# Attention inside a two-layer trunk: score matmuls in pairs of unlike row halves, values as the stationary operand, the softmax division ahead of the transposes

## The reference

```python
s_loc = jnp.einsum('bqgrd,bkgd->bgrqk', qb, kb).astype(jnp.float32) * scale
...
s_ctx = jnp.einsum('bqgrd,bkgd->bgrqk', qc, ck).astype(jnp.float32) * scale
p = jax.nn.softmax(jnp.concatenate([s_loc, s_ctx, sink_b], axis=-1), axis=-1)
o = (jnp.einsum('bgrqk,bkgd->bqgrd', p[..., :span].astype(v.dtype), vb)
     + jnp.einsum('bgrqk,bkgd->bqgrd', p[..., span:span + P].astype(cv.dtype), cv))
```

## Time and profile before

| | us |
|---|---|
| median of 3 runs | 1668.3 (1663.09 to 1668.85) |
| the profiled execution's own time | 1660.22 |
| its span | 1658.4 |
| mean granted PE clock | 0.91 of full speed |
| PE busy | 1321.3 (80% of the span) |
| DVE busy | 520.7 (31%) |
| ACT busy | 390.9 (24%) |
| POOL busy | 277.5 (17%) |

### The profile page before, as it was taken

One profiled execution on the slowest core, in us unless ns is written; L12 is line 12 of the kernel. 1 busy time (PEld: TensorE's weight loads), 2 busy tenths in 40 slices (PEclk: granted clock), 3 DMA queues, 4 the chain that ended last, 5 costly groups with the idle time before them and its releaser, 6 DMA issues.

```text
span 1658.4 us, 16936 instructions
## 1 busy us (share of the span) xinstructions
PE 1321.3 (80%) x6726; PEld 778.6 (47%) x6726; DVE 520.7 (31%) x1042; ACT 390.9 (24%) x753; POOL 277.5 (17%) x279
## 2 busy tenths in 40 slices
PE   3899989967996788989881799898699677787770
PEld 1455565545344344655440466565555444444430
DVE  3327542254123332121003285434622510000005
ACT  4311133211213122221123311332013311111113
POOL 4210010002000133232222026000000022222222
PEclk9899997988997699999995899899799679999995
DMA  9748110053555399999986021002000459999974
GB/s 347 254 158 285 53 54 26 26 191 130 190 175 209 125 415 419 395 415 381 394 365 228 0 76 55 0 26 83 32 0 39 177 204 417 400 412 407 406 297 195
DMA packets 71697, 350.90 MB, mean 212 GB/s; under 512 B 12925, under 2 KB 21755, under 8 KB 36680
## 3 DMA queue, kind: packets, MB, share of 16 engines
q1 hardware_dynamic: 56188, 316.78, 49.0%
q0 software_dynamic: 12704, 22.03, 3.7%
q10 hardware_dynamic: 2732, 11.08, 1.7%
HBM read 334.36 MB, written 31.20 MB: 220 GB/s over the span
## 4 chain that ended last, share of the span: by engine, by line
PE 57%; DMA 22%; DVE 11%; ACT 6%; issue 3%; SPq 0%; ACTq 0%; POOL 0%; POOLq 0%; DVEq 0%
DMA ring<-in_exp_up 17%; PE ps L1294 10%; PE ps L1241 9%; PE ps L1081 5%; PE ps L987 4%; PE ps L1309 3%; PE ps L1038 3%; PE ps L848 2%; PE ps L1008 2%; PE ps L1143 2%; DMA ring<-in_ada_w 2%; PE ps L1190 2%; PE ps L901 1%; PE ps L1221 1%; PE ps L1088 1%
## 5 line engine op out<-in xcount | busy, mean ns | idle before, releaser
L1294 PE MATMUL ps<-ring,work 128*64 128x256 f32 x2176 | 256.6, 389 | 47.6 <-DMA ring<-in_exp_up 44.5
L1294 PEld LDWEIGHTS ps<-ring,work 128*64 128x64 f32 x2176 | 173.2, 140 | 154.5 <-issue 95.3
L1309 PE MATMUL ps<-ring,work 128*64 128x512 f32 x544 | 133.5, 612 | 26.1 <-DVE work L2153 21.5
L1241 PE MATMUL ps<-ring,yT 128*128 128x512 f32 x320 | 145.2, 603 | 0.8 <-issue 0.8
L2151 DVE TENSOR_TENSOR work<-work,ps 64x256 f32<-64x256 f32 x56 | 23.8, 424 | 345.8 <-ACT work L1665 345.8
L780 POOL DMA_INDIRECT y_scratch<-work,tabs x56 | 57.7, 1030 | 337.1 <-ACT work L1672 337.1
L1911 DVE SCALAR_TENSOR_TENSOR work<-work,prmT 128x655 f32<-128x655 f32 x120 | 97.7, 891 | 0.0
L1241 PEld LDWEIGHTS ps<-ring,yT 128*128 128x128 f32 x320 | 59.5, 193 | 75.1 <-issue 75.0
L775 POOL DMA_INDIRECT work<-h_scratch,tabs x60 | 61.8, 1029 | 194.8 <-issue 157.2
L1081 PE MATMUL ps<-hT,ring 128*128 128x512 f32 x192 | 91.7, 622 | 0.3
L987 PE MATMUL ps<-hT,ring 128*128 128x512 f32 x128 | 68.0, 613 | 3.4 <-POOL hT L741 1.9
(11 more groups left out here) (375 smaller groups left out, 1886.3 us busy)
## 6 DMA issues: line engine op xcount, KB each, us to landing
ring<-in_exp_gate SPq DMA_DIRECT2D x68, 1024.0 KB, 8.1
ring<-in_exp_up SPq DMA_DIRECT2D x68, 1024.0 KB, 12.5
ring<-in_exp_down SPq DMA_DIRECT2D x68, 1024.0 KB, 11.8
ring<-in_ada_w SPq DMA_DIRECT2D x48, 1024.0 KB, 4.8
ring<-in_w_in SPq DMA_DIRECT2D x16, 1024.0 KB, 6.9
work<-y_scratch SPq DMA_DIRECT2D x10, 1024.0 KB, 6.8
ring<-in_w_out SPq DMA_DIRECT2D x8, 1024.0 KB, 6.3
k_scratch<-yT ACTq DMA_DIRECT2D x4, 1280.0 KB, 8.0
```

Of the source, the lines that this page charges most:

```text
L1241: last = mm(ps[:, (4, 6, 7, 0)[n % 4], :], yT[:, k, t * P:(t + 1) * P], wo[k // 2][:, k % 2, h * HALF:(h + 1) * HALF], start=(k == 0), sto ...
L1294: last = mm(ps[BR * q:BR * q + BR, 1, 0:FE], xe[:, s, kb, BR * h:BR * h + BR], w[:, q, k, :], start=(k == 0), stop=(k == KC - 1))
L1309: last = mm(ps[BR * h:BR * h + BR, 3, :], he[:, s, k, :], wd[:, k, HALF * h:HALF * h + HALF], start=(k == 0), stop=(k == 1))
```

## The change

- **Scores.** `score(i, h)` becomes `scores(i, m)`, which does the two heads m and m + 2 together: the matmul against the cached keys on rows 0 to 63, the same on rows 64 to 127, then the two against the rotated keys, again one on each half. Two of these pairs are placed behind the transposes of heads 2 and 3.
- **Values.** The values are stationary (128x64) and the transposed probabilities of two heads are streamed (256 columns). The matmul for key/value head 0 writes partitions 0 to 63 of bank 6, that for head 1 partitions 64 to 127; they alternate. The result is already transposed, so the two transposes of `otok`, `otok` itself and the semaphore `at_ot` are gone, and ACT copies `yT` from bank 6 after `at_pv`. PE waits for `yd_ok` ahead of the values, no longer ahead of head 1.
- **Division.** `divide(i)` on DVE now scales `prob` in place, per head, in two groups of two heads, before the transposes; these wait for `at_o` (20 per layer) in place of `at_exp`. It stands between `maximum(i)` and `outer_taps(i)`.
- **Output weights.** The heads now lie in another order in `yT`, so the last quarter of `w_out` is loaded in two DMAs of 64 partitions with its rows in that order, and `w_count` counts the extra one.

```diff
@@ out_unit (SP)
+                if j == 3:
+                    w = io["w_out"][l][3 * CH:4 * CH, :].rearrange("(g r d) n -> g d r n", g=2, r=2)
+                    for g in range(2):
+                        sp.dma_start(wbuf(OUT_U + j, 2, D)[g * HD:(g + 1) * HD], w[g]).then_inc(w_full[j % 4], 16)
+                    return
@@ PE
-                def score(i, h):
+                def scores(i, m):
                     if i > 0:
-                        pe.wait_ge(at_exp, nth(l, at_exp, 4 * (i - 1) + h + 1))
-                    p0, m = HD * (h // 2), h % 2
+                        pe.wait_ge(at_exp, nth(l, at_exp, 4 * (i - 1) + m + 3))
+                    lo, hi = max(i - 1, 0), min(i + 2, 4)
+                    for g in range(2):
+                        p0 = HD * g
+                        if i < 4:
+                            mm(ps[:, 2 * g + m, 0:P], qraw[p0:p0 + HD, m, i * P:(i + 1) * P], ckT[p0:p0 + HD, :],
+                               start=True, stop=True)
+                        else:
+                            mm(ps[:, 2 * g + m, 0:P], qraw[p0:p0 + HD, m, LS:T], kraw[p0:p0 + HD, LS:T],
+                               start=True, stop=True).then_inc(at_s, 1)
                     if i < 4:
-                        lo, hi = max(i - 1, 0), min(i + 2, 4)
-                        mm(ps[:, h, 0:P], qraw[p0:p0 + HD, m, i * P:(i + 1) * P], ckT[p0:p0 + HD, :], start=True, stop=True)
-                        last = mm(ps[:, h, P:P + (hi - lo) * P], qrope[p0:p0 + HD, m, i * P:(i + 1) * P],
-                                  krope[p0:p0 + HD, lo * P:hi * P], start=True, stop=True)
...
+                        for g in range(2):
+                            p0 = HD * g
+                            mm(ps[:, 2 * g + m, P:P + (hi - lo) * P], qrope[p0:p0 + HD, m, i * P:(i + 1) * P],
+                               krope[p0:p0 + HD, lo * P:hi * P], start=True, stop=True).then_inc(at_s, 1)
...
                     for h in range(4):
-                        pe.wait_ge(at_exp, nth(l, at_exp, 4 * i + h + 1))
-                        if h == 1 and i > 0:
-                            pe.wait_ge(yd_ok, nth(l, yd_ok, i))
+                        pe.wait_ge(at_o, nth(l, at_o, 4 * i + h + 1))
                         if h >= 2:
                             pe.wait_ge(at_te, nth(l, at_te, 4 * i + h - 1))
                         for t in range(nk):
                             last = tr(ps[:, 4 + h % 2, t * P:(t + 1) * P], prob[:, h, t * P:(t + 1) * P], ident)
                         last.then_inc(at_t, 1)
-                        if i + 1 < NT:
-                            score(i + 1, h)
+                        if i + 1 < NT and h >= 2:
+                            scores(i + 1, h - 2)
                     hyena_tile(i + 1, 0, 4)
-                    for h in range(4):
-                        kv = h // 2
-                        pe.wait_ge(at_te, nth(l, at_te, 4 * i + h + 1))
-                        for t in range(nk):
+                    pe.wait_ge(at_te, nth(l, at_te, 4 * i + 4))
+                    if i > 0:
+                        pe.wait_ge(yd_ok, nth(l, yd_ok, i))
+                    for t in range(nk):
+                        for kv in range(2):
...
-                            last = mm(ps[:, 6, h * HD:(h + 1) * HD], probT[:, h, t * P:(t + 1) * P], v,
+                            last = mm(ps[kv * HD:(kv + 1) * HD, 6, 0:2 * P], v, probT[:, 2 * kv:2 * kv + 2, t * P:(t + 1) * P],
                                       start=(t == 0), stop=(t == nk - 1))
                     last.then_inc(at_pv, 1)
                     hyena_tile(i + 1, 4, KC)
-                    pe.wait_ge(at_o, nth(l, at_o, i + 1))
-                    for q in range(2):
-                        last = tr(ps[:, 5, q * P:(q + 1) * P], otok[:, q * P:(q + 1) * P], ident)
-                    last.then_inc(at_ot, 1)
@@ ACT
-                    act.wait_ge(at_ot, nth(l, at_ot, i + 1))
-                    A(yT[:, 6:8, i * P:(i + 1) * P], ps[:, 5, 0:2 * P].rearrange("p (q t) -> p q t", q=2), ACT.Copy) \
+                    act.wait_ge(at_pv, nth(l, at_pv, i + 1))
+                    A(yT[:, 6:8, i * P:(i + 1) * P], ps[:, 6, 0:2 * P].rearrange("p (q t) -> p q t", q=2), ACT.Copy) \
@@ DVE, divide(i)
-                    dve.wait_ge(at_exp, nth(l, at_exp, 4 * i + 4))
-                    step(V.tensor_tensor(ast[:, i % 2, 6, :], ast[:, i % 2, 3, :], ast[:, i % 2, 4, :], ALU.add))
-                    step(V.reciprocal(ast[:, i % 2, 7, :], ast[:, i % 2, 6, :]))
-                    dve.wait_ge(at_pv, nth(l, at_pv, i + 1))
-                    V.tensor_tensor(otok.rearrange("p (h c) -> p h c", h=4), ps[:, 6, 0:256].rearrange("p (h c) -> p h c", h=4),
-                                    bc(ast[:, i % 2, 7, :], HD), ALU.mult).then_inc(at_o, 1)
+                    nk = (3, 4, 4, 3, 1)[i]
+                    for a in (0, 2):
+                        dve.wait_ge(at_exp, nth(l, at_exp, 4 * i + a + 2))
+                        step(V.tensor_tensor(ast[:, i % 2, 6, a:a + 2], ast[:, i % 2, 3, a:a + 2], ast[:, i % 2, 4, a:a + 2],
+                                             ALU.add))
+                        step(V.reciprocal(ast[:, i % 2, 7, a:a + 2], ast[:, i % 2, 6, a:a + 2]))
+                        for h in (a, a + 1):
+                            V.tensor_scalar(prob[:, h, 0:nk * P], prob[:, h, 0:nk * P], ast[:, i % 2, 7, h:h + 1], None,
+                                            ALU.mult).then_inc(at_o, 1)
@@ DVE, the loop
                 outer_taps(0)
+                divide(0)
                 for i in range(NT):
                     if i + 1 < NT:
                         maximum(i + 1)
-                    divide(i)
+                        divide(i + 1)
                     outer_taps(i + 1)
```

More of the change, by code:

```diff
@@ L193, in trunk @@
         probT = at(work, 3584, 4, 512)
-        otok = at(work, 5632, 256)
         u = ([yT[:, 2 + c, :] for c in range(2)] + [at(ring[:, 5, :], i * T, T) for i in range(3)]
@@ L357, in trunk @@
         at_o = sem("at_o")
-        at_ot = sem("at_ot")
         yd_ok = sem("yd_ok")
@@ L459, in trunk @@
             (at_mm, 5), (at_ev, 8), (at_rot, 3), (at_rope, 3), (kv_out, 32), (at_s, 20), (at_max, 5), (at_exp, 20),
-            (at_t, 20), (at_te, 20), (at_pv, 5), (at_o, 5), (at_ot, 5), (yd_ok, 5),
+            (at_t, 20), (at_te, 20), (at_pv, 5), (at_o, 20), (yd_ok, 5),
             (hy_lay, 3), (hy_phase, 2), (hy_sine, 2), (hy_f, 10), (hy_raw, 10), (hy_abs, 10), (hy_eo, 10), (hy_norm, 2),
@@ L483, in w_count @@
         def w_count(l, j):
-            return 16 * (2 + 3 * l + j // 4)
+            return 16 * (2 + 3 * l + j // 4) + 16 * ((j % 4 == 3) * l + (j == OUT_U + 3))
         apos = [(4, 5, 0, 1, 2, 3)[p] if p < 6 else 4 if 24 <= p < 32 else 4 + p % 2 for p in range(24 * DEPTH)]
@@ L1098, in _ @@
                 pe.wait_ge(hy_uc, nth(l, hy_uc, 1))
-                def score(i, h):
+                def scores(i, m):
                     if i > 0:
-                        pe.wait_ge(at_exp, nth(l, at_exp, 4 * (i - 1) + h + 1))
-                    p0, m = HD * (h // 2), h % 2
-                    if i < 4:
-                        lo, hi = max(i - 1, 0), min(i + 2, 4)
-                        mm(ps[:, h, 0:P], qraw[p0:p0 + HD, m, i * P:(i + 1) * P], ckT[p0:p0 + HD, :], start=True, stop=True)
-                        last = mm(ps[:, h, P:P + (hi - lo) * P], qrope[p0:p0 + HD, m, i * P:(i + 1) * P],
-                                  krope[p0:p0 + HD, lo * P:hi * P], start=True, stop=True)
-                    else:
-                        last = mm(ps[:, h, 0:P], qraw[p0:p0 + HD, m, LS:T], kraw[p0:p0 + HD, LS:T], start=True, stop=True)
-                    last.then_inc(at_s, 1)
-                for h in range(4):
-                    score(0, h)
+                        pe.wait_ge(at_exp, nth(l, at_exp, 4 * (i - 1) + m + 3))
[8 more added lines that the diff above has]
+                               start=True, stop=True).then_inc(at_s, 1)
+                    if i < 4:
+                        for g in range(2):
+                            p0 = HD * g
+                            mm(ps[:, 2 * g + m, P:P + (hi - lo) * P], qrope[p0:p0 + HD, m, i * P:(i + 1) * P],
+                               krope[p0:p0 + HD, lo * P:hi * P], start=True, stop=True).then_inc(at_s, 1)
+                for m in range(2):
+                    scores(0, m)
                 hyena_tile(0, 4, KC)
```

## The result

| | before | changed |
|---|---|---|
| median of 4 runs each, us | 1666.38 (1663.09 to 1668.85) | 1642.39 (1636.03 to 1643.22) |
| ratio, 95% interval | | 0.9846 (0.9823 to 0.987) |
| span of the profiled execution | 1658.4 | 1640.8 |
| PE busy | 1321.3 | 1288.5 |
| DVE busy | 520.7 | 535.1 |

The change is 24.0 us faster; 20.9 had been forecast. The time itself, 1642.4 us, lies 5.0 under the forecast 1647.4: 3.1 of it is this gain, 1.9 the base, since the forecast started from a median of 1668.3. The profile of before had been taken on an execution some 6 us under its median, so the difference of the two spans, 17.6 us, is less than the difference of the medians.

A forecast was written before the change was run, and what follows sets the result against it. PE was taken to bound the attention loop; values 4.95, scores and transposes 3.1 and the loop's start 2.4 us make 10.4 a layer, 20.9 for two: 1668.3 - 20.9 = 1647.4 us, range 1638 to 1660.

The forecast's parts named there:

- What bounds: In the attention loop PE is the bound, busy 79.15 of 82.0 us; later stages follow when the loop ends earlier.
- The values: In each round, column halves run at once, four key blocks taking 2.1 us against 3.52; gain 4.95 us a layer.
- The charge of 0.3 us a round: Around each round's values, changing between full and half array costs 0.15 us twice.
- Scores and transposes: In rounds 1 to 4, pairs of scores gain 1.55, 1.1, 0.45 and 0 us, 3.1 us a layer.
- The new wait: In rounds 1 to 3, PE waits some 0.9 us for ACT's copy of head 0 before head 2's transposes.
- Heads 1 and 2 of tile 0: In tile 0 they take 0.77 us together, head 0 alone 0.73, so a pair costs one head.
- The start of the loop: At low clock before the first hyena tile, which starts 2.4 us earlier; gain 2.4 us a layer, low end 1.2.
- The later start: At the loop's start, the first transposes wait for exponentials, sum, reciprocal and first scaling, starting 1.2 us later.
- What was hidden: DVE's scalings are covered by 2.5 us in round 1; the second DMA for `w_out` costs 0.
- The clock didn't fall inside the rounds: Rival: the clock falls in each round's transposes and scores, about 6 us in four rounds of two layers; 1695 us, 5%.
- The halves of the columns run at once: Rival to this: the values' halves run singly, 0.22 us an instruction, four blocks 3.8 us; 1660 us in all, 4%.
- wait for scaled probabilities: Rival: PE waits 1.3 us ahead of each of four rounds, two layers, costing about 10 us; 1658 us, 9%.

The follow-up runs named there:

- like_halves: The changed kernel with pairs made of heads 0 and 1, then 2 and 3, so both scores lie on the same row half; 1662.4 us.
- pairs_only: The kernel before with only the scores in pairs of unlike row halves, behind the transposes of heads 2 and 3; 1651.2 us.
- no_division: The changed kernel without DVE's sums, reciprocals and scalings, so output not normalised; 1671.5 us, not comparable; loops 78.6 and 79.6 us.

## Why the prediction was right, and where its terms were off

- **What bounds.** Right inside the loops: what PE's rows gained there is what the loops gained. What stands behind them followed, but for 3.6 us: the loops gained 27.6 us, the medians 24.0. The forecast of 20.9 missed the loops by 6.7 and the total by only 3.1, because these 3.6 us went the other way; that nearness is luck.
- **The values.** Forecast 4.95 us a layer. Measured in layer 1: 13.1 us before (2.62 + 3.52 + 3.52 + 2.62 + 0.84), 7.24 now, gain 5.9, less 0.6 that the hyena halves around them grew (3.54 to 3.63, and 3.49 to 3.54), so 5.3. The charge of 0.3 us a round for changing the form of the array was too high; 0.14 was paid beside the values, and at four key blocks 0.08 within them (1.88 against 16 x 0.1125).
- **Scores and transposes.** Forecast 1.55, 1.1, 0.45, 0, sum 3.1; measured 1.59, 1.16, 0.50, 0, sum 3.25. The new wait, forecast at some 0.9, is 0.85 (0.96 in round 3). Heads 1 and 2 of tile 0 were the right row: a pair costs 1.07 us in round 1, and with both scores on one half 1.94 (`like_halves`).
- **The start of the loop.** Forecast 2.4 us, measured 6.0 in layer 0 and 4.5 in layer 1. The later start was forecast at 1.2 us and is 1.4. The step that failed is "The clock rose 4.2 us after the hyena tile began. If it keeps that distance, all 2.4 us are kept": the clock did not wait for the hyena tile. With the scores in pairs on unlike halves it rose 1.5 and 0.5 us before that tile, and the low stretch shrank from 17 to 7 and 10 us. In the kernel before the distance was 4.3 us in one layer and 3 in the other, so it was no constant there either. This term was the largest error, 3.6 and 2.1 us, and its range had no end on that side. (A slip in the range itself: 0.3 us in five rounds of two layers are 3.0, not 2.7.)
- **What was hidden.** Right: the first scaling ends 1.8 us before PE needs it (2.5 had been forecast), the outer taps hold nothing up that they did not before (round 4's block is 2.60 us, as before), and the second DMA costs nothing in the stretch of layer 0 that was compared. The division delays the first transposes by 1.41 us, but leaving it out shortens the loop by 0.6 us at most.
- **The rivals.** The clock didn't fall inside the rounds: 1.00 in every window of 2 us in the changed kernel's rounds. It did in one loop of `like_halves`, so such a fall exists beside scores on single halves; it cost 1.7 us each time, where the prediction had priced it at 6. The halves of the columns run at once: every one of the values' instructions has its own weight load, and 16 of them take 1.88 us, 0.12 each, where one alone takes 0.22. The Trainium skill ("TensorE: Matmul & The Clock Gate", Part 3, "What overlaps and what doesn't") says that a weight load overlaps with running matmuls only when the row groups differ. These have the same rows, so for this form the trace differs from it, and the trace decides. No wait for scaled probabilities appeared behind the start.

## What to carry to other kernels

Two matmuls that contract over 64 rows cost one if they stand next to each other on unlike halves of the rows, and the same holds for stationary operands of 64 columns whose outputs lie on unlike halves of the partitions: look for the unlike neighbour in the trace you have, and alternate them. Place such a pair where it also covers another engine's copy, and look first what the pair itself has to wait for. Where a stretch begins at low clock, an earlier start may buy little (here 0.6 of 1.4 us at most); the pairs bought more there than the matmuls they saved, since the low clock ended earlier.

## What was not expected of the hardware

- With the same transposes, later start and hyena tiles around the scores, the clock was low for 17 to 21 us with the scores on single halves of the rows (`like_halves`) and for 7 to 10 us with them in pairs on unlike halves (the changed kernel). The kernel before and `pairs_only` differ in the same way, 17 against 10.
- PE starts matmuls out of the program's order if their half of the array is free, about four instructions ahead: 2.80 us for 16 instructions in turn, 1.88 alternating, 16 x 0.22 = 3.5 if they had run one by one.
- A block started 1.41 us earlier at low clock took 1.01 us longer in layer 1: 0.55 us was a wait for ACT's copy, and most of the rest the clock, which rose at the same distance from the first scores (`no_division`).
